# 512-column matmuls that stream their weights, and write their output, from the last column to the first

## The reference

```python
for i in range(DEPTH):                              # DEPTH = 2
    xn = rmsnorm(h, g_mix[i])
    # layer 0: sparse attention + differential attention, one input and one output projection
    # layer 1: RG-LRU block, one input projection of 4096 columns and one output projection
    h = h + mix
    h = h + swiglu(rmsnorm(h, g_ffn[i]), w_ffn_gate[i], w_ffn_up[i], w_ffn_down[i])   # D_FF = 5632
    gate = jax.nn.sigmoid(rmsnorm(h, g_ple[i]) @ w_ple_gate[i])
    h = h + gate * (p[i] @ w_ple_proj[i])           # p[i]: 256 x 256
return rmsnorm(h, g_final)
```

## Time and profile before

| | |
|---|---|
| median of three runs | 2471.91 us |
| profiled execution | 2473.23 us |
| its span, from first to last instruction | 2471.5 us |
| granted TensorE clock, mean | 0.997 |
| PE busy | 2445.6 us, 99%, 11084 matmuls |
| DVE busy | 1315.4 us, 53% |
| ACT busy | 1139.5 us, 46% |
| HBM traffic | 443.87 MB, 180 GB/s |

### The profile page before, as it was taken

How to read it: one execution, slowest core, us unless ns; L and a number is a source line. 1 busy time by engine, 2 the same in 40 slices (tenths; PEclk the granted TensorE clock), 3 DMA queues, 4 the chain that set the end, 5 groups by cost and what they waited for, 6 DMA issues and landing times.

```text
span 2471.5 us, 29756 instructions
## 1 busy us (share of the span) xinstructions
PE 2445.6 (99%) x11084; PEld 1994.7 (81%) x11084; DVE 1315.4 (53%) x1677; ACT 1139.5 (46%) x1533; POOL 3.2 (0%) x17
## 2 busy tenths in 40 slices
PE   8999999999999999999999999999999999999997
PEld 7888778888888888888888888888888888888886
DVE  5545665555454454444566676554454454444455
ACT  5435555544444444444454575544444444344454
POOL 0000000000000000000000000000000000000000
PEclk9999999999999999999999999999999999999999
DMA  7744435666666665555557445566666666555563
GB/s 215 229 120 120 131 117 182 185 187 186 187 187 182 186 186 184 187 188 187 187 187 235 140 154 178 186 183 185 187 187 184 186 183 188 186 187 187 187 204 135
DMA packets 234042, 443.87 MB, mean 180 GB/s; under 512 B 16184, under 2 KB 21344, under 8 KB 233824
## 3 DMA queue, kind: packets, MB, share of 16 engines
q1 hardware_dynamic: 233904, 442.62, 58.7%
q10 hardware_dynamic: 48, 0.02, 0.0%
HBM read 440.49 MB, written 2.10 MB: 179 GB/s over the span
## 4 chain that ended last, share of the span: by engine, by line
PE 96%; DVE 1%; ACT 1%; DMA 1%; issue 0%; ACTq 0%; DVEq 0%
PE ps L1278 30%; PE ps L1276 30%; PE ps L1277 30%; PE ps L1232 2%; PE ps L1487 1%; PE ps L1400 1%; PE ps L1331 1%; DMA raw<-in_w_in_rec_dram 1%; DVE w_lo L774 0%; ACT w_hi L537 0%; PE ps L1412 0%; PE ps L1437 0%; ACT prob L691 0%; DMA h<-in_x_dram 0%; PE ps L1371 0%
## 5 line engine op out<-in xcount | busy, mean ns | idle before, releaser
L774 DVE TENSOR_TENSOR w_lo<-raw,w_hi 128x1024 fp32r<-128x1024 f32 x820 | 998.4, 1220 | 1071.1 <-ACT w_hi L537 1070.1
L537 ACT ACTIVATE w_hi<-raw 128x1024 fp32r<-128x1024 f32 x820 | 863.1, 1055 | 1137.3 <-PE ps L1278 1108.2
L1278 PE MATMUL ps<-w_hi,xa_lo 128*128 128x512 f32 x1664 | 656.9, 395 | 0.0
L1277 PE MATMUL ps<-w_lo,xa_hi 128*128 128x512 f32 x1664 | 654.2, 393 | 0.0
L1276 PE MATMUL ps<-w_hi,xa_hi 128*128 128x512 f32 x1664 | 653.9, 393 | 0.0
L1277 PEld LDWEIGHTS ps<-w_lo,xa_hi 128*128 128x128 f32 x1664 | 312.7, 188 | 73.1
L1276 PEld LDWEIGHTS ps<-w_hi,xa_hi 128*128 128x128 f32 x1664 | 312.6, 188 | 70.5
L1278 PEld LDWEIGHTS ps<-w_hi,xa_lo 128*128 128x128 f32 x1664 | 312.6, 188 | 68.8
L1276 PE MATMUL ps<-w_hi,xb_hi 128*128 128x512 f32 x864 | 351.3, 407 | 3.9 <-DVE xb_lo L837 2.3
L1278 PE MATMUL ps<-w_hi,xb_lo 128*128 128x512 f32 x864 | 341.9, 396 | 0.0
L1277 PE MATMUL ps<-w_lo,xb_hi 128*128 128x512 f32 x864 | 341.0, 395 | 0.0
(11 more groups left out here) (200 smaller groups left out, 1043.9 us busy)
## 6 DMA issues: line engine op xcount, KB each, us to landing
raw<-in_w_ffn_gate_dram SPq DMA_DIRECT2D x176, 512.0 KB, 3.6
raw<-in_w_ffn_up_dram SPq DMA_DIRECT2D x176, 512.0 KB, 3.6
raw<-in_w_ffn_down_dram SPq DMA_DIRECT2D x176, 512.0 KB, 3.6
raw<-in_w_in_attn_dram SPq DMA_DIRECT2D x88, 512.0 KB, 3.7
raw<-in_w_ple_gate_dram SPq DMA_DIRECT2D x64, 512.0 KB, 3.8
raw<-in_w_in_rec_dram SPq DMA_DIRECT2D x64, 512.0 KB, 4.3
raw<-in_w_out_attn_dram SPq DMA_DIRECT2D x32, 512.0 KB, 3.7
raw<-in_w_out_rec_dram SPq DMA_DIRECT2D x32, 512.0 KB, 3.7
```

Of the source, the lines that this page charges most:

```text
L537: nc.scalar.activation(w_hi[:, s, 0:n], raw[:, s, 0:n], ACT.Copy).then_inc(hi_ready, 1)
L774: nc.vector.tensor_tensor(w_lo[:, s, 0:n], raw[:, s, 0:n], w_hi[:, s, 0:n].bitcast(F32), ALU.subtract).then_inc(lo_ready, 1)
L1277: nc.tensor.matmul(o, xh[:, k, tok], w_lo[:, s, wk], start=False, stop=False)
L1278: ins = nc.tensor.matmul(o, xl[:, k, tok], w_hi[:, s, wk], start=False, stop=(k == nkt - 1))
```

## The change

In the branch of `multiply_slot` for 512 columns both the moving operand and the output get an access pattern that starts at the last column and steps back by one element, `[:, ::-1]`. Column c of the weights still lands in column c of the bank. The stationary operand, the order of the matmuls, their waits and their counts stay. On each engine the instructions stand in the same order as before; only the step and the start of the two patterns differ (step 1 becomes step -1, the start moves by 511 elements). After the change the three matmuls stand on lines 1277 to 1279 instead of 1276 to 1278.

```diff
                 for m in range(NT):
-                    o = ps[:, EX + m if ple_p else 2 * r + m, c0:c0 + w]
+                    o = ps[:, EX + m if ple_p else 2 * r + m, c0:c0 + w][:, ::-1]
                     for k in range(k0, k0 + nk):
                         tok = slice(m * P, (m + 1) * P)
                         wk = slice((k - k0) * w, (k - k0 + 1) * w)
-                        nc.tensor.matmul(o, xh[:, k, tok], w_hi[:, s, wk], start=(k == 0), stop=False)
-                        nc.tensor.matmul(o, xh[:, k, tok], w_lo[:, s, wk], start=False, stop=False)
-                        ins = nc.tensor.matmul(o, xl[:, k, tok], w_hi[:, s, wk], start=False,
-                                               stop=(k == nkt - 1))
+                        wh, wl = w_hi[:, s, wk][:, ::-1], w_lo[:, s, wk][:, ::-1]
+                        nc.tensor.matmul(o, xh[:, k, tok], wh, start=(k == 0), stop=False)
+                        nc.tensor.matmul(o, xh[:, k, tok], wl, start=False, stop=False)
+                        ins = nc.tensor.matmul(o, xl[:, k, tok], wh, start=False, stop=(k == nkt - 1))
                 ins.then_inc(w_used, 1)
```

## The result

The changed kernel takes 2496.01 us (median of three runs, 2493.97 to 2496.35) against 2471.91: ratio 1.009, 95% interval 1.0073 to 1.0107. It is slower by 24 us, nearly 1%. The profiled execution took 2493.97 us, its span 2492.2.

A forecast was written before the change was run, and what follows sets the result against it. PE's matmul pace was taken as the bound: 9792 x 0.231 = 2262 us, 91% of the span. Issue, read and write each added 0 to 2473, giving 2472 as a measured median; 8 in 10 range 2420 to 2535.

The forecast's parts named there:

- what bounds the kernel: On PE: start-to-start matmul pace 0.231 us times 9792 matmuls, 2262 us or 91% of the span.
- The slack that I read from ACT's waits: ACT and DVE split weights, then idle; ACT waits 1108 us for PE, so any new pace passes to the end undiluted.
- issue and semaphores: Cost term for instructions and waits around the matmuls: none added or moved, so nothing.
- the output write: Cost term for the descending write into the bank: neighbours still share 8-byte PSUM lines, taken as 0.
- rival 1: All 9792 matmuls lose column pairing, falling to one column per 1.2 GHz cycle, 0.427 us each: 4392 us; chance 0.14.
- a descending read still fetches its elements together: Moving read: 512 neighbouring elements, four hits per 16-byte line, so free by the skill's rule.
- the mean over the ring: Moving read's stalls: single slots may shift 3 to 6 ns, but the mean pace stays, 0 ns with 1 ns either side.
- rival 2: Moving read meets the weight load more often; all slots at 0.2327 us, +17 us, 2490, or 2523 at three times; chance 0.16.
- the case held likeliest: Mean matmul pace kept: 2472 us, own range 2462 to 2482; chance 0.50.
- the prediction's own sign: Test on the matmul pace: the forecast is wrong if its mean moves by over 1 ns.
- collisions with the weight load: Explanation of 17 ns per matmul above 0.2135 us: moving read and next weights' load meet in the same memory; inferred.

The follow-up runs named there:

- e3_fwd_d0: Kernel before (ascending), ring rows 1024 elements apart and w_hi, w_lo moved so every slot has distance 0 (modulo 256 bytes) from the stationary operand; 2436.63 us, ratio 0.9852.
- e11_x_moved_d0: Kernel before (ascending), ring rows 1024 elements apart, distance 0 reached by moving the stationary operands xa, xb, hid instead of the weights; 2434.47 us, ratio 0.9847.
- e1_write_only: Changed kernel with the weights read ascending again, so only the output write descends and pieces land mirrored; 2472.7 us, ratio 1.000.
- e12: Kernel before (ascending), placed so that w_hi lies at distance 0 from the stationary operand and w_lo at distance 128; 2474.76 us (one run).
- e6: Kernel before (ascending), with the four ring places at distances 0, 32, 64 and 96 bytes from the stationary operand; 2478.77 us (one run).
- e7: Kernel before (ascending), with the four ring places at distances 128, 160, 192 and 224 bytes from the stationary operand; 2493.61 us (one run).

## Why the prediction was partly right

*Right: what bounds the kernel.* The pace times 9792, with hardly anything diluting it. The loss of 24 us is the 2.5 ns of pace to within the 2 us left over above, PE's waits did not grow, and of the 4.1 x 9792 = 40 us that the pace promises in e3_fwd_d0 and e11_x_moved_d0, 37 came through in each, against the runs of the kernel before that were timed with them (1.5%). The slack that I read from ACT's waits is real, but not everywhere: in e3_fwd_d0 PE waits 1.8 us for the split weights, against 0.6 before.

*Right: issue and semaphores at nothing, the output write at nothing.* e1_write_only shows the second by itself. The Trainium skill (PSUM — Partial Sum Buffer, Specifications (TRN2)) has any non-contiguous pattern slow a matmul significantly. By e1_write_only a step of -1 over all 512 columns of a bank costs nothing within 0.1%. So the rule does not hold for this step, and rival 1 with its 4392 us is out.

*Right as far as it shows: a descending read still fetches its elements together.* The pace did not fall to 0.427, and at 1.2 GHz it stayed there, as forecast. But the rule that I quoted for it (the Trainium skill, Advanced Engine Details and Errata, Memory Cachelines: enough hits on a line and the access is at full performance) gives no cost for the direction, and the measurement has one, 2.5 ns here and 6.6 at the best distance. The measurement decides.

*Wrong: the mean over the ring.* The step that failed is "If turning the direction does no more than to meet the weight load in another phase, the mean stays where it is", with its 0 ns. It supposed that a descending read has good and bad alignments in the same mixture. It has no good one among ten. What the kernel before had was a half share of a good one: places 1 and 3 at distance 64, 2.75 us a slot, 0.2292. The change takes that away. Half the matmuls lose 0.2333 - 0.2292 = 4.1 ns, the other half 0.2333 - 0.2325 = 0.8, in the mean 2.5 ns. That is rival 2, which had 0.16 and was priced at 2490 for all slots at the pace of the slow ones: right in place and sign, 6 us short, as the common pace is 0.2333 and not 0.2327. That the descending read meets the weight load more often, which was rival 2's reason, is not shown. So the case held likeliest (2462 to 2482) did not come, and by the prediction's own sign ("wrong if the pace moves by over 1 ns in the mean") the forecast of the pace failed: it moved by 2.5. The stretches had the 216 matmuls that it had given to rival 2. That 2496 lies within 2420 to 2535 is no merit of the main argument, but of the room that was left for the rivals.

*Wrong as an explanation: collisions with the weight load in proportion to it.* I had called it inferred. The dependence on the distance between both operands stands (e3, e11, e12), but a half or a quarter of the loaded columns changes the pace by 0.5 ns or less. What gives 13 to 23 ns a matmul (0.2267 to 0.2367 against 0.2135), whether it lies in the memory at all, why that depends on the distance, and why the descending read settles at 0.2333 at nine of ten distances, stays open. No run has a descending read of the stationary operand, which would be the obvious further test.

## What to carry to other kernels

Where the matmul pace is the bound, measure it from start to start in one pure stretch and compare it with the columns divided by the clock; an excess that differs between ring slots of equal work points to addresses. Lay the moving and the stationary operand out so that all slots have the same good distance (here equal modulo 256 bytes: 1.5% of the whole kernel for a change of three numbers in the layout), and pad rings by a multiple of that period rather than by part of it. Before one argues that a mean over alignments is kept, the new pattern's pace has to be known at one alignment at least.

## What the runs showed of the hardware that was not expected

- A 512-column float32r matmul at 2.4 GHz followed the last at 0.2267, 0.2292 or about 0.233 us depending on the distance of its operands modulo 256 bytes; 0.2135 was never reached in a long stretch, while at 1.2 GHz 0.427 was met exactly, ascending and descending (12.48 to 14.19 us of the changed kernel).
- Distances that are odd multiples of 32 bytes were as bad as 128 and 192 (e6, e7), and the cost of one matmul's distance is borne by its successors (e12: 0.2311 where 0.229 was due; e6: nine matmuls at 0.231 before the tenth and the next go at 0.2267).
- The direction of the output write has no price (ratio 1.000, 0.9991 to 1.0009), that of the moving read has one, 2.4% of the time at distance 0 (2495.28 against 2436.63).
